# Expert routing inside the residual loop, fixed slots per expert, and expert rows scattered back to token order

## The reference, cut to what matters

```python
x = x + g1 * rmsnorm(y, norm_post_mix)              # y: mixed heads @ w_out
h = rmsnorm(x, norm_pre_ffn) * (1.0 + sc2) + sh2
lg = h @ w_rg + b_rg                                 # 4 groups
grp = argmax(lg); gate_g = softmax(lg)[grp]
le = (einsum('td,gde->tge', h, w_re) + b_re)[grp]    # 8 experts of the group
top_v, top_i = top_k(le, 2)
w_top = softmax(top_v) * gate_g
expert = grp * 8 + top_i                             # 2 of 32 for each token
# rows grouped by expert, in blocks of 128 rows:
hid = silu(xb @ w_gate[e]) * (xb @ w_up[e])          # 1024 -> 512
yb = hid @ w_down[e]                                 # 512 -> 1024
out[token] += yb * w_top
x = x + g2 * rmsnorm(out, norm_post_ffn)
```

## Time and profile before

| what | value |
|---|---|
| time, median of 3 runs | 2875.59 us (2873.09 to 2876.07) |
| span of the profiled execution | 2866.6 us |
| median less that span (before the first and behind the last instruction) | 9.0 us |
| PE busy | 2353.3 us, 82% |
| DVE, ACT, POOL busy | 52%, 35%, 20% |
| mean granted TensorE clock | 0.905 of full |
| DMA | 517.35 MB, mean 180 GB/s |

### The profile page before, as it was taken

The page is one execution under the profiler, slowest core; times in us unless marked ns, Lnnn a source line. Parts: engine busy times, 40 slices in busy tenths (PEclk is TensorE's granted clock), DMA queues, the critical chain, the costliest instruction groups (busy, mean ns, idle before and its releaser), DMA issues. The chain is left out here.

```text
span 2866.6 us, 36466 instructions
## 1 busy us (share of the span) xinstructions
PE 2353.3 (82%) x11872; PEld 1934.3 (67%) x11873; DVE 1478.6 (52%) x1668; ACT 1008.4 (35%) x1343; POOL 569.1 (20%) x610
## 2 busy tenths in 40 slices
PE   4899989999994636878769991499999999999850
PEld 2788869989993225766658881377777777787740
DVE  2333331100103866999974444066576656546858
ACT  2433333222211311111122221066566656546732
POOL 0000000000001346666621104210010000001126
PEclk8899999999986869999989995699999999999985
DMA  7222241121125869433324334378697777658969
GB/s 255 69 88 88 100 156 45 48 84 44 45 75 169 311 216 330 169 140 142 140 84 150 137 126 107 118 245 296 234 308 242 270 274 242 223 201 292 362 224 367
DMA packets 296544, 517.35 MB, mean 180 GB/s; under 512 B 35249, under 2 KB 209457, under 8 KB 292273
## 3 DMA queue, kind: packets, MB, share of 16 engines
q1 hardware_dynamic: 261168, 394.52, 40.1%
q0 software_dynamic: 19200, 63.49, 6.3%
q10 hardware_dynamic: 16128, 58.73, 5.1%
HBM read 407.99 MB, written 108.69 MB: 180 GB/s over the span
## 5 line engine op out<-in xcount | busy, mean ns | idle before, releaser
L2101 DVE TENSOR_TENSOR e_w_low<-e_w_whole,e_w_high 128x2048 fp32r<-128x2048 f32 x186 | 417.9, 2289 | 128.8 <-ACT e_w_high L2054 128.8
L2054 ACT ACTIVATE e_w_high<-e_w_whole 128x2048 fp32r<-128x2048 f32 x186 | 345.5, 1909 | 44.7 <-DVE e_y L2119 44.7
L2007 PE MATMUL e_pG<-e_w_high,e_xT 128*128 128x512 f32 x768 | 305.4, 398 | 1.2 <-ACT e_xT L2047 1.2
L2008 PE MATMUL e_pG<-e_w_low,e_xT 128*128 128x512 f32 x768 | 305.2, 397 | 0.0
L602 PE MATMUL proj_acc<-w_high,hT_high 128*128 128x512 f32 x672 | 272.8, 406 | 6.9 <-DVE hT_low L637 5.7
L602 PE MATMUL proj_acc<-w_low,hT_high 128*128 128x512 f32 x672 | 268.4, 399 | 0.0
L602 PE MATMUL proj_acc<-w_high,hT_low 128*128 128x512 f32 x672 | 267.9, 399 | 0.0
L2026 PE MATMUL e_pY<-e_w_high,e_hT 128*128 128x512 f32 x768 | 226.1, 407 | 0.0
L2011 PE MATMUL e_pG<-e_w_high,e_xT 128*128 128x512 f32 x768 | 194.7, 395 | 0.0
L2007 PEld LDWEIGHTS e_pG<-e_w_high,e_xT 128*128 128x128 f32 x768 | 145.2, 189 | 36.8 <-issue 1.6
L2008 PEld LDWEIGHTS e_pG<-e_w_low,e_xT 128*128 128x128 f32 x768 | 145.4, 189 | 35.2
(11 more groups left out here) (286 smaller groups left out, 4567.3 us busy)
## 6 DMA issues: line engine op xcount, KB each, us to landing
e_w_whole<-in_moe_w_gate_dram SPq DMA_DIRECT2D x64, 1024.0 KB, 7.1
e_w_whole<-in_moe_w_up_dram SPq DMA_DIRECT2D x64, 1024.0 KB, 10.4
e_w_whole<-in_moe_w_down_dram SPq DMA_DIRECT2D x64, 1024.0 KB, 7.5
rows_done<-e_y ACTq DMA_DIRECT2D x48, 512.0 KB, 6.7
m_tok<-by_token SPq DMA_DIRECT2D x16, 1280.0 KB, 6.8
xt<-in_x_dram SPq DMA_DIRECT2D x32, 512.0 KB, 5.6
wm_rest<-in_w_mod_dram POOLq DMA_DIRECT2D x8, 2048.0 KB, 12.0
by_token<-tok SPq DMA_DIRECT2D x16, 768.0 KB, 5.6
```

Of the source, the lines that this page charges most:

```text
L2007: nc.tensor.matmul(pG[:, half], xT[:, 0, k], wh[:, half, w], start=(k == 0), stop=False)
L2008: nc.tensor.matmul(pG[:, half], xT[:, 0, k], wl[:, half, w], start=False, stop=False)
L2054: nc.scalar.activation(wh[:, third, part], raw[:, third, part], ACT.Copy).then_inc(whs.sem, 1)
L2101: nc.vector.tensor_tensor(wl[:, third, part], raw[:, third, part], wh[:, third, part].bitcast(F32), ALU.subtract).then_inc(wls.sem, 1)
```

## The change

The routing stage is gone. Its work is done per tile inside the residual loop, which is now written out for all tiles on every engine, with stages one, two and three tiles further back: DVE's `choose(t-2)` and `place(t-3)`, two Exp of ACT and two products of TensorE (four in the last tile) for tile t−3, and two scatters of GpSimd for tile t−4. Experts have fixed slots: expert e's rows begin at e x 2048 of `ids`, which now holds two numbers for each slot, the token to gather and the row to write; `ids` is filled with "none" at the stage's start. Starts need not be known, so ranks can be given tile by tile. The experts' rows are scattered to token order (row k x 2048 + token) by GpSimd two blocks later, instead of being stored by ACT, and combine reads them with plain loads on SP. The space of the experts' raw weights is kept from the convolution stage on (w_out lies in it during mixing and residual), so that expert 0's weights are loaded during the residual loop; their split moves to the start of the experts stage.

```diff
 # residual, sync
+            sp.dma_start(iota[:], io["iota8"]).then_inc(o_in.sem(0), 16)
+            sp.dma_start(row[:], io["tokens"]).then_inc(o_in.sem(0), 16)
...
-            for t, use, s in pairs(sp, 2, NL):
+            for t in range(2, NL):
                 sp.wait_ge(yTt.sem, yTt.at(t - 2))
-                load_y(t, use, s)
+                load_y(t, t // 2, t % 2)
                 sp.wait_ge(x1s.sem, x1s.at(t - 2))
-                load_x(t, use, s)
+                load_x(t, t // 2, t % 2)
+                if t == 3:
+                    sp.wait_ge(wls.sem, wls.at(KD - 1))
+                    for third in range(3):
+                        load_third(sp, io, g["e_raw"], 0, third, g["e_w_in"].sem(third))
 # residual, gpsimd: ids filled with "none", constants; then in body(t), between the two roots
+                if there(t - 4):
+                    r = t - 4
+                    pool.wait_ge(step.sem, placed_at(r, NB))
+                    for k in range(2):
+                        pool.indirect_dma_start(dram["ids"], bass.IndirectOffsetOnAxis(ap=g["slots"][:, k, r:r + 1], axis=0), token[:, r, k], None).then_inc(ids_out.sem(0), 16)
 # residual, tensor, at the end of body(t)
+                if there(t - 3):
+                    pe.wait_ge(step.sem, chosen_at(r, NA))
+                    pe.wait_ge(step.sem, placed_at(r - 1, NB))
+                    nc.tensor.matmul(pr[:, 0:NE], g["tri"][:, 3], both[:, r % 2], start=True, stop=False)
+                    nc.tensor.matmul(pr[:, 0:NE], g["tri"][:, 4], summed[:], start=False, stop=True).then_inc(ranked.sem, 1)
 # residual, scalar, at the start of body(t)
+                    act.wait_ge(step.sem, chosen_at(r, NA))
+                    nc.scalar.activation(e4[:, r % 2], d4[:, r % 2], ACT.Exp, accum_out=den[:, r % 2]).then_inc(asked.sem, 1)
+                    nc.scalar.activation(ex[:, r % 2], v8[:, r % 2, 0:1], ACT.Exp, bias=v8[:, r % 2, 1:2], scale=-1.0).then_inc(asked.sem, 1)
 # residual, vector, at the end of body(t): link() makes each step wait for the one before
+            def choose(r):                       # 2 adds, then 15 links
+                V.tensor_tensor(l8[:, s, 0:NG], pl[:, 0:NG], br[:, 0:NG], ALU.add).then_inc(lgs.sem, 1)
+                V.tensor_tensor(le[:].rearrange("p a b -> p (a b)"), pl[:, NG:NG + NE], br[:, NG:NG + NE], ALU.add).then_inc(lgs.sem, 1)
+                link(V.max(m8[:], l8[:, s]))
+                link(V.max_index(i8[:], m8[:], l8[:, s]))
...
+                link(V.tensor_tensor(both[:, s], oh[:, s, 0], oh[:, s, 1], ALU.add))
+            def place(r):                        # 8 links, 10 in the last tile
...
+                link(V.tensor_copy(g["slots"][:, :, r], sl[:]))
-                    nc.vector.tensor_tensor(g["logits"][:, bass.ds(t - 2, 1)].rearrange("p o n -> p (o n)"), pl[:, 0:NG + NE], br[:], ALU.add).then_inc(lgs.sem, 1)
+                    choose(t - 2)
+                if there(t - 3):
+                    place(t - 3)
-def routing(nc, kit, io, g, dram):
...
 # experts, gpsimd
+            nc.gpsimd.memset(ids[:], SKIP).then_inc(none.sem, 1)
+            nc.gpsimd.memset(held[:], SKIP).then_inc(none.sem, 1)
+            nc.gpsimd.memset(y[:], 0.0).then_inc(none.sem, 1)
+            pool.wait_ge(none.sem, none.at(0))
+            pool.indirect_dma_start(dram["ys"], bass.IndirectOffsetOnAxis(ap=held[:, 1:2], axis=0), y[:], None, bounds_check=2 * SEQ - 1, oob_is_err=False).then_inc(y_out.sem(0), 16)
+            def advance(b):
+                pool.wait_ge(y_out.sem(0), b * 16 + 16)
+                nc.gpsimd.tensor_copy(held[:, 1:2], held[:, 0:1]).then_inc(held_on.sem, 1)
+                pool.wait_ge(held_on.sem, held_on.at(b))
+                nc.gpsimd.tensor_copy(held[:, 0:1], ids[:, 1:2]).then_inc(taken.sem, 1)
+                pool.wait_ge(taken.sem, taken.at(b))
+            def scatter(b):
+                pool.wait_ge(ya.sem, b + 1)
+                pool.wait_ge(yd.sem, b + 1)
+                pool.indirect_dma_start(dram["ys"], bass.IndirectOffsetOnAxis(ap=held[:, 1:2], axis=0), y[:], None, bounds_check=2 * SEQ - 1, oob_is_err=False).then_inc(y_out.sem(0), 16)
             def load(b, row, following):
+                advance(b)
                 pool.wait_ge(xTt.sem, xTt.at(b - 1))
...
                 gather()
+                scatter(b)
 # experts, scalar (DVE's copy waits in the same way)
-                act.wait_ge(y_out.sem(0), b * 16 + 16)
+                act.wait_ge(y_out.sem(0), b * 16 + 48)
                 nc.scalar.activation(y[:, 0:512], pY[:, 0], ACT.Copy).then_inc(ya.sem, 1)
-                act.wait_ge(ya.sem, ya.at(b))
-                act.wait_ge(yd.sem, yd.at(b))
-                act.dma_start(dram["ys"][bass.ds(row, P), :], y[:]).then_inc(y_out.sem(0), 16)
...
+            high(0, 0)
+            high(0, 1)
             xT_copy(0)
+            high(0, 2)
 # combine, gpsimd: only the roots are left; sync
             def load(t):
+                if t >= B:
+                    sp.wait_ge(summed.sem, summed.at(t - B))
+                for k in range(2):
+                    sp.dma_start(yy[:, t % B, k], dram["ys"][k * SEQ + t * P:k * SEQ + (t + 1) * P, :]).then_inc(y_in.sem(t % B), 16)
                 if t >= B:
                     sp.wait_ge(outs.sem, outs.at(t - B))
                 sp.dma_start(x1[:, t % B], dram["x1"][t]).then_inc(x_in.sem(t % B), 16)
```

More of the change, by code:

```diff
@@ new lines, in place @@
+            def place(r):
+                s = r % 2
+                if r == 0:
+                    dve.wait_ge(ruled.sem, ruled.at(0))
+                dve.wait_ge(asked.sem, asked.at(r))
+                link(V.scalar_tensor_tensor(out=dn[:], in0=ex[:, s], scalar=1.0, in1=den[:, s], op0=ALU.add, op1=ALU.mult))
+                link(V.reciprocal(g["wtop"][:, 0, r:r + 1], dn[:]))
+                link(V.tensor_tensor(g["wtop"][:, 1, r:r + 1], g["wtop"][:, 0, r:r + 1], ex[:, s], ALU.mult))
+                dve.wait_ge(ranked.sem, ranked.at(r))
+                if r == NL - 1:
+                    dve.wait_ge(counted.sem, counted.at(0))
+                link(V.tensor_tensor(summed[:], summed[:], both[:, s], ALU.add))
+                link(V.tensor_tensor(rank[:], pr[:, 0:NE], first[:], ALU.add))
+                link(V.tensor_tensor(wr2[:], oh[:, s], rank[:].unsqueeze(1).to_broadcast([P, 2, NE]), ALU.mult))
+                link(V.tensor_reduce(sl[:], wr2[:], AX, ALU.add))
+                link(V.tensor_copy(g["slots"][:, :, r], sl[:]))
+                if r == NL - 1:
+                    link(V.tensor_scalar(nb[:], pr[0:1, NE:2 * NE], 1.0, float(P - 1), ALU.max, ALU.add))
+                    link(V.tensor_single_scalar(g["blocks"][:], nb[:], 7, ALU.arith_shift_right))
@@ L1878, in experts @@
     with ExitStack() as st:
[L1879 to L1880 removed]
+        raw = g["e_raw"]
+        wh = kit.sb("e_w_high", [P, 3, THIRD], F32R, stack=st)
+        wl = kit.sb("e_w_low", [P, 3, THIRD], F32R, stack=st)
+        ids = kit.sb("e_ids", [P, 2], I32, stack=st)
+        held = kit.sb("e_rows_held", [P, 2], I32, stack=st)
         xb = kit.sb("e_x", [P, D], stack=st)
@@ L1975, in _ @@
             gather()
+            scatter(b)
+            advance(b + 1)
+            scatter(b + 1)
+            pool.wait_ge(y_out.sem(0), b * 16 + 48)
+            pool.sem_inc(junk.sem, 1)
         @block.tensor
@@ L2148, in _ @@
         def _(pool):
-            def gather(t):
-                if t >= B:
-                    pool.wait_ge(summed.sem, summed.at(t - B))
-                for k in range(2):
-                    pool.indirect_dma_start(yy[:, t % B, k], None, dram["ys"], bass.IndirectOffsetOnAxis(ap=g["slots"][:, k, t:t + 1], axis=0)).then_inc(y_in.sem(t % B), 16)
-            def root(t):
+            for t in range(NL):
                 pool.wait_ge(ssq.sem, ssq.at(t))
                 rstd_root(nc, g, pool, eps_added, t, 1, ss[:, t % B, 1:2], ss[:, t % B, 0:1], D).then_inc(rstd.sem, 1)
-            for t in range(NL + 2):
-                if t < NL:
-                    gather(t)
-                if t >= 2:
-                    root(t - 2)
         @block.sync
@@ L2235, in program @@
         g[part] = kit.sb(part, [P, 4, KD, 512], F32R, stack=first_only)
-    for stage in (modulation, projection, convolution, states, mixing, residual, routing, experts, combine):
+    for stage in (modulation, projection, convolution, states, mixing, residual, experts, combine):
         if stage is convolution:
```

318 lines of the change are left out of this document (137 added, 181 removed).

## The result

The kernel after takes 2901.32 us, the median of 4 runs (2894.26 to 2905.18); beside it on the same chip the kernel before took 2875.83 (4 runs, 2873.09 to 2877.56). The ratio is 1.0089, 95% interval 1.0072 to 1.0106: slower, by more than the 0.2% that can be told from no change. The prediction was 2900. The kernel after was run once more, later, in six runs: 2893.91, ratio 1.0071 (1.0055 to 1.0087).

The account below looks back on a forecast made before the run. TensorE was taken to bound residual and experts, a chain of small steps the gap, DVE the combine stage. −53 + 11 + 17 − 18 + 68 = +25: span 2892, time 2900; 8-in-10 range 2866 to 2935.

Parts of the forecast that it names:

- the likeliest case: Whole kernel: the forecast as summed, +25 us, span 2892, time 2900; chance 0.62.
- The gap: Tile 15's last product to first turned block: new chain ends at E+63.6 instead of E+117.0, −53 us.
- E: Residual stage: the time when a tile's last product ends, from which the steps of the chain are counted.
- The residual loop: Residual tiles: DVE's added small operations delay h2, pitch 15.5, 0.84 more on 13 tiles, +11 us.
- Expert 0's weights: SP's queue in the residual stage: y of tile 4 waits behind the weights, TensorE stands once, +17 us.
- The experts: Experts stage: ACT no longer waits for DVE's half or stores, shortening TensorE's e_hid waits, −18 us.
- Rival C: Experts: GpSimd's chain becomes the pace, TensorE waits some 1 us per block; 2940 middle, 2965 worst; chance 0.12.
- The combine stage: Combine: rows asked for only when finish(t−2) ends, 10.5 us a tile, 164.6 against 96.6, +68 us.
- L: Combine: time from finish's end until the second 512 KB has landed, behind a store; taken as 5.9 us.
- A: Combine: the three transfers overlap, L = 3.5, total −9, time 2866; chance 0.13.
- B: Combine keeps DVE's pace if loads can run ahead; about −46, time 2830; chance 0.05.
- D: Residual loop: GpSimd's scatters held by DVE operations, root 2 us late, pitch 17, +20 more, 2920; chance 0.08.

Follow-up runs that it names:

- e5: Kernel after with GpSimd's memsets and a small DMA replacing the empty scatter moved into the residual stage, DVE clearing y: 2878.64 us, ratio 1.0014.
- e11: Kernel after with the edits of e1, e3 and e5, plus an unused 2784-byte tensor in front of yT in the residual stage: 2785.57 us, ratio 0.9683.
- e3: Kernel after with expert 0's six weight loads issued behind y and x of the last tile instead of tile 3: 2877.10 us, ratio 1.0000.
- e4: Kernel after with ACT again waiting for DVE's half of y before splitting the third part of the next weights: 2908.42 us, ratio 1.0109.
- e1: Kernel after with SP asking for combine's row loads of tile t before waiting for the result of tile t-2: 2825.00 us, ratio 0.9821.

## Why the prediction was right, and where by luck

**The forecast's mechanism** was the right one in each part but the residual loop, where the chain was not the limit, and the likeliest case came: +25 on the profiled execution predicted, +35.6 measured there, of which 9.2 is the spread of the untouched stages, so +26.4 for the touched ones. That the sum came within 1.4 is luck: combine cost 14.8 more than predicted, and the residual loop with the weights (6.1 less), the experts (6.9 better) and the gap (0.4 better) made that up. In the profile taken later combine is +78.6, and the touched stretches sum up to +18.8 against +25. The median of 2900 was as lucky: the first four runs gave 2901.3, the six later ones 2893.9.

**The base.** The prediction says of the median that it "is 9.0 longer, and I carry that over". The table of the time before takes this as time around the span, and that reading was wrong: what lies around the span is 1.6 us, and the execution profiled before was a short one, by some 6 to 8 us. Carrying it over was still right, since the kernel after has that spread too.

**The gap**, −53, measured −53.4. The prologue was taken as 6 and measured as 7.7 to the first fetch; removing it gave 9.5 (e5). The steps up to the last scatter came out at E+34.9 against E+34.4.

**The residual loop**, +11: `choose` took 3.8 us for 17 steps, 0.22 each, as estimated from the earlier trace rows. But ACT's square was done at E+9.9 and not E+10.5, h2 was ready at E+14.6 and not E+15.4, so the chain ended just before TensorE wanted h2: pitch 15.12, all of the growth being the rank product's 0.45. That is 6 on 13 tiles, and not 11. The step that failed is the sum along the chain, 0.8 us too much, in a place where 0.4 decided. e11 shows the other side: with products 0.3 a tile shorter, the same chain ends 0.16 too late for it.

**Expert 0's weights**, +17: 13.7 measured, and 16.2 with the low clock behind it (e3). The mechanism (y behind 6.3 MB in one queue) stands. The six loads took 24.6 us from the first issue to the last landing, not 28.4; the clock behind the stall, which the sum left out, makes up for it, and that is luck too.

**The experts**, −18: −24.9. The cause named is shown for 16.5 (e4); the clock, which the text put only into the bound, gave 5.5. Rival C fell: GpSimd did wait 257.9 us for its scatters, but all of it beside TensorE.

**The combine stage**, +68: +82.8 in this execution, 77 to 80 in the others. The mis-sized term is L, 5.9 taken, 6.9 measured (6.5 to 6.6 in the others), inside its bounds of 3.5 and 7.5; the first `finish` ended 13.8 us after the stage's start and not 12.1, another 1.7. L was read from two loads beside a store in the residual stage, where the DMA engines are less loaded (0.36 against 0.54 here); that this makes the difference was not tried. The Trainium skill's fit ("DMA: Bandwidth & Descriptors", "Anatomy of one DMA — SWDGE (gpsimd) path") gives 5.6 for 1.5 MB and 4.4 for 1 MB, estimates for one transfer of GpSimd's path; measured here, on SP's queue and with the issues in it, are 6.5 to 6.9 for the three and 4.7 for the two alone, so the trace lies above the fit, little for two and more for three.

**Rivals.** A needed L at or below 4.1; even the two loads alone cost 4.7. B (DVE keeps the pace) is what e1 nearly makes, by the edit that the change lacks; its price of −46 does not follow from the terms, 25 less 68 is −43. D came in part: 13 of the 32 scatters took 1.6 to 2.0 us, each beside one of DVE's two operations on h2, the others 1.0 to 1.1; but the pitch of 15.12, which is TensorE's own work, shows that they held nothing. The Trainium skill ("GPSIMD Engine Reference", "Specifications") says that GpSimd suffers from VectorE's instructions with two SBUF inputs; these 13 scatters agree, and cost nothing on the path.

## What to carry to other kernels

A load that takes the place of a prefetching gather must keep its lead: look at what its issue waits for, and compare that with the wait of the very instruction that will need it. A queue that serves a loop's inputs is the wrong place for a large transfer that nobody needs yet; behind the last input it costs nothing. Compare executions by stage: here 16 us in one stage (e4) hid in a total that moved by 7, and 9 us in untouched stages, within their spread of 12, looked like a cost.

## What the runs showed of the hardware that I had not expected

The pace of a float32 product of 512 columns at the full clock depends on where its two operands lie to each other in a partition: 0.2333 us with 102432 or 102464 bytes from the start of the moving operand's tensor (the high weights) to that of the stationary one, 0.2268 with 102400, 106496 or, in the residual stage, 86016 (before and after it was 83232 there, and 0.2333). The fast ones are multiples of 4096, but multiples of 512 are enough, as the single products of a row show. That is 2.8% of TensorE's time in a stage that it bounds: 12 to 13 us of 914. Why the distance matters, no run shows. Two kernels that differ by one small unused tensor can so differ by 0.4%, and an edit that moves an allocation has this effect with its own.

Two 512 KB loads issued together took 4.7 us from the release of the queue to the use of both, of which 0.8 are their issue; with a store and a third load right behind them 5.9, with the store ahead 6.5 to 6.9.
